# The end of a decoder step on one core: one tile's residual to GpSimd, the samples' output to GpSimd, and the last tile's additions in another order

## The reference

```python
xp = xp + mp[5] * hierarchical_moe(modulate(xp, norm_ffn_g[l], mp[3], mp[4]), ...)
xs = xs + ms[5] * hierarchical_moe(modulate(xs, norm_ffn_g[l], ms[3], ms[4]), ...)
```

## Time and profile before

| | |
|---|---|
| median of 3 runs | 760.4 us (759.92 to 761.41) |
| the profiled execution, span | 768.8 us |
| TensorE busy | 739.2 us (96%) |
| VectorE busy | 409.4 us (53%) |
| ScalarE busy | 205.8 us (27%) |
| GpSimd busy | 171.1 us (22%) |
| mean granted TensorE clock | 0.990 |
| read from and written to memory | 180.89 MB and 16.13 MB |

### The profile page before, as it was taken

How to read it: one execution, slowest core, us unless ns; L and a number is a source line. 1 busy time by engine, 2 the same in 40 slices (tenths; PEclk the granted TensorE clock), 3 DMA queues, 4 the chain that set the end, 5 groups by cost and what they waited for, 6 DMA issues and landing times.

```text
span 768.8 us, 11131 instructions
## 1 busy us (share of the span) xinstructions
PE 739.2 (96%) x4235; PEld 464.7 (60%) x4235; DVE 409.4 (53%) x942; ACT 205.8 (27%) x418; POOL 171.1 (22%) x193
## 2 busy tenths in 40 slices
PE   7999999999999999998999999989999999999986
PEld 5445465688756567885888444656555555555541
DVE  4124399998999998600254235974432232222235
ACT  5012253306467675002000011222111111111112
POOL 2031021240000000073400004543333333333210
PEclk9999999999999999998999999989999999999999
DMA  8973064113255275443232842377999999999988
GB/s 339 419 254 97 0 218 159 46 78 115 109 220 220 110 256 207 143 166 138 80 116 83 344 179 92 139 260 286 423 423 425 427 424 423 426 426 422 423 332 321
DMA packets 29385, 187.72 MB, mean 244 GB/s; under 512 B 7264, under 2 KB 8352, under 8 KB 17936
## 3 DMA queue, kind: packets, MB, share of 16 engines
q1 hardware_dynamic: 18880, 164.98, 53.9%
q0 software_dynamic: 9536, 19.72, 7.8%
q10 hardware_dynamic: 912, 2.26, 0.8%
HBM read 180.89 MB, written 16.13 MB: 256 GB/s over the span
## 4 chain that ended last, share of the span: by engine, by line
PE 75%; DVE 9%; DMA 8%; issue 3%; ACT 2%; SPq 1%; POOL 1%; DVEq 0%; ACTq 0%; POOLq 0%
PE psum L810 23%; PE psum L1302 13%; PE psum L777 12%; PE psum L1316 7%; DMA ring<-in_experts 5%; PE psum L724 3%; PE psum L1295 2%; DMA ring<-in_stream 2%; PE psum L670 2%; DMA ring<-expert_rows 1%; DVE arena L2284 1%; DVE arena L2282 1%; DVE arena L2283 1%; PE psum L653 1%; PE psum L1309 1%
## 5 line engine op out<-in xcount | busy, mean ns | idle before, releaser
L810 PE MATMUL psum<-hT,ring 128*128 128x260 f32 x640 | 146.7, 389 | 5.3 <-issue 3.3
L810 PEld LDWEIGHTS psum<-hT,ring 128*128 128x128 f32 x640 | 121.9, 192 | 29.5 <-issue 8.5
L1785 ACT ACTIVATE arena<-psum 128x512 f32<-128x512 f32 (+10 forms) x127 | 68.3, 573 | 234.8 <-PE psum L653 50.9
L777 PE MATMUL psum<-ring,hT 128*128 128x512 f32 (+1 forms) x256 | 93.1, 517 | 0.0
L777 PEld LDWEIGHTS psum<-ring,hT 128*128 128x128 f32 x256 | 47.4, 190 | 41.8 <-issue 32.6
L1302 PE MATMUL psum<-ring,arena 128*64 128x256 f32 x608 | 69.0, 379 | 2.2 <-DMA ring<-in_experts 1.2
L1316 PE MATMUL psum<-arena 128*64 128x512 f32 x280 | 67.8, 605 | 1.4 <-issue 1.4
L1717 POOL DMA_INDIRECT expert_rows<-arena,router x34 | 34.5, 1014 | 140.0 <-DVE arena L2784 127.7
L1302 PEld LDWEIGHTS psum<-ring,arena 128*64 128x64 f32 x608 | 43.8, 137 | 31.3 <-issue 10.3
L2777 DVE COPY arena<-psum 128x128 f32<-128x128 f32 x35 | 10.2, 291 | 95.6 <-PE psum L1309 83.8
L810 PE MATMUL psum<-arena,ring 128*128 128x260 f32 x256 | 58.9, 386 | 0.0
(11 more groups left out here) (398 smaller groups left out, 962.5 us busy)
## 6 DMA issues: line engine op xcount, KB each, us to landing
ring<-in_stream SPq DMA_DIRECT2D x21, 2048.0 KB, 8.9
ring<-in_experts SPq DMA_DIRECT2D x16, 2048.0 KB
arena<-in_experts SPq DMA_DIRECT2D x32, 1024.0 KB
arena<-in_experts SPq DMA_DIRECT2D x11, 2048.0 KB
hT<-in_experts SPq DMA_DIRECT2D x5, 2048.0 KB
ring<-expert_rows SPq DMA_DIRECT2D x8, 512.0 KB, 7.2
ring<-in_stream SPq DMA_DIRECT2D x2, 1280.0 KB, 6.1
arena<-in_x_prompt SPq DMA_DIRECT2D x4, 512.0 KB, 5.7
```

Of the source, the lines that this page charges most:

```text
L777: mm = pe.matmul(psum[:, b, 0:width], hT[:, k, t * P:(t + 1) * P], w[:, k, :], start=(k == 0), stop=(k == KD - 1))
L810: mm = pe.matmul(psum[:, b0 + s, 0:HALF], w[:, k, f * P:(f + 1) * P], rhs[:, k, s * HALF:(s + 1) * HALF], start=(first and k == 0), stop=( ...
L1785: ins = act.activation(out, in_, func, scale=scale)
```

## The change

- TensorE: the residual of tile 1 no longer goes through PSUM; its sums start with the first one-hot matmul. The residual half in the wait for `y_out` is now one of tile 2.
- ScalarE copies tile 1's sums to `last_sums`, free space in `hT`, so that `x2[:, 1, :]` keeps the residual.
- GpSimd, behind its overflow loop, adds `picked[1][1]` to `x2[:, 1, :]`; VectorE adds `last_sums` to `picked[0][1]`, waits for GpSimd, and adds `x2[:, 1, :]`.
- VectorE: in the last tile, the PSUM sums and the second choices are added first, as soon as both are there, and then, in two halves, the first choices.
- GpSimd waits for its scatter, loads the samples' two choices, does the three small operations and stores `y_s`; then it waits for that store. SyncE no longer does any of this, and VectorE neither.
- Two semaphores are shared with others than before.

```diff
@@ TensorE
             down(LAST_P, w_dn[k], y_full)
-            last_residual(1, 0)
+            last_residual(2, 0)
             pe.wait_ge(last_hot_ready, 3)
             pe.wait_ge(y_out, N_MAIN)
             last_tile(0)
-            last_residual(1, 1)
+            banks.begin(pe, ("last", 1), LAST_BANK[1], LAST_BANK[1] + 1)
             last_tile(1)
-            for h in range(2):
-                last_residual(2, h)
+            last_residual(2, 1)
             last_tile(2)
@@ last_rows
-                                 start=False, stop=True)
+                                 start=(t == 1), stop=True)
@@ SyncE
-                if t == 1:
-                    sp.wait_ge(*s_scattered)
-                    for c in range(2):
-                        sp.dma_start(s_cols[:, 2 + c, :], sample_columns(by_token[c, SEQ:TOK, :])).then_inc(s_picked[0], 16)
...
-            sp.wait_ge(*y_s_ready)
-            sp.dma_start(sample_columns(io["y_s"]), s_cols[:, 2, :]).then_inc(y_outs, 16)
-            sp.wait_ge(y_outs, 16 * (T5 + 1))
+            sp.wait_ge(y_outs, 16 * T5)
@@ GpSimd, behind over_pairs
+            pool.wait_ge(*picked_in[1][1])
+            lane.mark(pool.tensor_tensor(x2[:, 1, :], x2[:, 1, :], picked[1][1], ALU.add))
+            x2_picked.append(lane.count)
+            pool.wait_ge(*s_scattered)
+            for c in range(2):
+                pool.dma_start(s_cols[:, 2 + c, :], sample_columns(by_token[c, SEQ:TOK, :])).then_inc(s_picked[0], 16)
+            a, gate2, x = s_cols[:, 2, :], s_cols[:, 0, :], s_cols[:, 1, :]
+            pool.wait_ge(*s_back)
+            pool.wait_ge(*s_picked)
+            lane.then(pool.tensor_tensor(a, a, s_cols[:, 3, :], ALU.add))
+            lane.then(pool.tensor_tensor(a, a, gate2, ALU.mult))
+            lane.then(pool.tensor_tensor(a, a, x, ALU.add))
+            store(sample_columns(io["y_s"]), a)
             pool.wait_ge(outs, 16 * n_outs[0])
@@ ScalarE
-                evac(("last", t), [(halves(x2[:, t, :]), psum[:, LAST_BANK[t]:LAST_BANK[t] + 2, :])])
+                sums = last_sums if t == 1 else x2[:, t, :]
+                evac(("last", t), [(halves(sums), psum[:, LAST_BANK[t]:LAST_BANK[t] + 2, :])])
@@ VectorE
-            for t in range(NT):
-                picks_summed(t)
-                if t < NT - 1:
-                    last_added(t)
+            picks_summed(0)
+            last_added(0)
+            dve.wait_ge(*picked_in[0][1])
+            banks.wait_drained(dve, ("last", 1))
+            lane.then(dve.tensor_tensor(picked[0][1], picked[0][1], last_sums, ALU.add))
+            dve.wait_ge(pool_lane, x2_picked[0])
+            dve.tensor_tensor(picked[0][1], picked[0][1], x2[:, 1, :], ALU.add).then_inc(y_ready, 1)
+            picks_summed(2)
+            last_added(2)
+            t = NT - 1
+            dve.wait_ge(*picked_in[1][t])
+            for h in range(2):
+                banks.wait_drained(dve, ("last", t, h))
+            lane.then(dve.tensor_tensor(x2[:, t, :], x2[:, t, :], picked[1][t], ALU.add))
+            dve.wait_ge(*picked_in[0][t])
             for h in range(2):
                 cols = slice(512 * h, 512 * h + 512)
-                banks.wait_drained(dve, ("last", t, h))
-                if h == 0:
-                    lane.wait()
                 dve.tensor_tensor(picked[0][t][:, cols], picked[0][t][:, cols], x2[:, t, cols], ALU.add).then_inc(y_ready, 1)
-
-            a, gate2, x = s_cols[:, 2, :], s_cols[:, 0, :], s_cols[:, 1, :]
-            dve.wait_ge(*s_back)
-            dve.wait_ge(*s_picked)
-            lane.then(dve.tensor_tensor(a, a, s_cols[:, 3, :], ALU.add))
-            lane.then(dve.tensor_tensor(a, a, gate2, ALU.mult))
-            dve.tensor_tensor(a, a, x, ALU.add).then_inc(y_s_ready[0], 1)
```

More of the change, by code:

```diff
@@ L432, in decoder_step @@
         s_cols = at(19456, 4 * Q_S).rearrange("p (m n) -> p m n", m=4)
+        last_sums = hT.rearrange("p k n -> p (k n)")[:, 0:D]
         last_hot = at(20992, NT * P).rearrange("p (t n) -> p t n", t=NT)
@@ L500, in decoder_step @@
         s_kept = (c_in, 16 + 32)
-        const2_in = sem("const2_then_s_picked_in")
-        s_picked = (const2_in, 32 + 32)
+        const2_in = sem("const2_in")
         bias_gain_in = sem("bias_gain_in_then_spread_moved")
@@ L533, in decoder_step @@
         x2_in = [(sem("x2_0_in"), 16), (ln_in, 32), (ws_in, 32), (pages_in, 32), (pages_all_in, 32)]
-        router_in = sem("router_in")
+        router_in = sem("router_then_s_picked_in")
+        s_picked = (router_in, 32 + 32)
         x2_half, x2_ready = sem("x2_half"), sem("x2_ready")
@@ L580, in decoder_step @@
         max_s_ready, probs_s_ready = sem("max_s_ready"), sem("probs_s_ready")
-        new_spread_ready = sem("new_spread_then_y_s_ready")
-        y_s_ready = (new_spread_ready, 2)
+        new_spread_ready = sem("new_spread_ready")
         merged = sem("merged")
@@ L585, in decoder_step @@
         vector_lane, scalar_lane, pool_lane = sem("vector_lane"), sem("scalar_lane"), sem("pool_lane")
-        n_outs = [0]
+        n_outs, x2_picked = [0], []
         last_use = {}
```

## The result

The changed kernel is slower: 773.27 us median of 17 runs against 763.56 us for the kernel before on the same chips, ratio 1.0126 (95% interval 1.0107 to 1.0145), that is 9.6 us more (8.2 to 11.1). The forecast was 11.4 us more: right in sign and in cause, and 1.8 us too large. As a time it was 771.8 us, only 1.5 us from the measured one, and that closeness is luck: it was added to the 760.4 us of three runs, which lie 3.2 us under the median of all 17.

The account below looks back on a forecast made before the run. It took the end to be bound by the prompt's last half and the samples, within 0.2 us. `y_s` at 770.1 plus GpSimd's uncovered drain gave +11.4 us; added to 760.4 that is 771.8 us, range 760.5 to 775.0.

Parts of the forecast that it names:

- the sum: Kernel's end: `y_s` lands at 770.1, then GpSimd's whole drain, to 780.2 us, 11.4 over the profiled 768.8.
- the blocked VectorE addition: Tile 1's first VectorE addition, held by GpSimd's; claimed to end 1.06 us behind it, at 759.8.
- The drain: GpSimd's close: the whole 9.64 us, as fixed work over all issued, runs uncovered behind `y_s`; chance 0.53.
- rival (a): GpSimd's close: the drain settles something for 4.7 us behind the last landing; +6.3, 766.7 us; chance 0.12.
- (b): GpSimd's close: the drain costs nothing when the queue is empty; +1.7, 762.1 us; chance 0.24.
- The sample path: End of GpSimd: sample loads, three additions and store land `y_s` at 770.1, about 1.7 us later than before.
- The collision: Tile 1: GpSimd's and VectorE's additions don't run side by side; VectorE's halves end at 766.1, 0.7 us later.
- its twin: GpSimd's 1024-wide addition in the router stage, 2.35 us, taken as the length of the new one.
- The gain: TensorE about 2 us shorter; the last tile's new order alone gains VectorE 1.3 us.

Follow-up runs that it names:

- e10: The kernel before plus one wait: GpSimd waits for all stores of y before it closes; ratio 1.0114 to the kernel before.
- e9: The changed kernel with two early GpSimd drains in idle stretches, behind the load of `b_router` and behind the last full scatter; ratio 1.0011 to the kernel before.
- e4: The changed kernel, but SyncE stores `y_s` once GpSimd's last operation is done; ratio 1.0103 to the kernel before.
- e7: The changed kernel with two early GpSimd drains, before the wait for the tables and behind the last full scatter; ratio 1.0059 to the kernel before.
- e1: The kernel before with only the samples' loads, sums and store moved to GpSimd; ratio 1.0141 to the kernel before.
- e5: The changed kernel with 64 more one-element transfers issued by GpSimd in an idle stretch; ratio 1.0135 to the kernel before.
- e6: The changed kernel with one early GpSimd drain, before the wait for the tables; ratio 1.0097 to the kernel before.
- e3: The changed kernel with samples back on SyncE and VectorE, and VectorE adding tile 1's residual instead of GpSimd; ratio 0.9990 to the kernel before.
- e2: The changed kernel with the samples given back to SyncE and VectorE, GpSimd's 1024-wide addition kept; ratio 1.0007 to the kernel before.

## Why the prediction was right

| term of the sum, us | predicted | measured |
|---|---|---|
| VectorE's last half ready, against before | +0.7 | +0.45 |
| GpSimd's addition / the blocked VectorE addition | 2.35 / ends 1.06 behind it | 2.89 / ends 1.08 behind it |
| last half's store to landing | 2.7 | 2.1 |
| second sample load landed, behind the scaling | 13.2 | 12.4 |
| three operations on GpSimd, to the store's issue | 1.7 | 2.6 |
| store of `y_s` to landing | 2.5 | 1.8 |
| `y_s` landed, behind the scaling | 17.4 | 16.8 |
| closing drain | 9.65 | 8.07 |
| TensorE's last matmul, against before | -2 | -2.1 |
| end of the span, against before | +11.4 | +9.5 |

**The drain.** The step that carried the forecast, that the 9.64 us of the earlier trace rows are work over what was issued and not a wait, held: e10 shows it with nothing of the change, e9 by taking it away. The prediction chose this reading by elimination, from one row, and gave it 0.53; and its range, 760.5 to 775.0 us, took in rival (a) and most of (b), so the runs, and not the time in the range, bear it out. Its size was the mis-sized term, by 1.6 us. The prediction called it work over all that was issued, and in that it was wrong: with three transfers more the drain was shorter, 8.07 us against 9.30 in e10, and with 64 more on top it stayed so. Why is open. Rival (a) read the 4.7 us behind the scatter's landing in the kernel before as a settlement; e4 refutes it. Rival (b), the free drain, is what e7 and e9 make of it when they leave four transfers: then the end is 1.5 to 1.6 us later than before by the trace, a ratio of 1.002; timed, e9 has 1.0011, and e7 1.0059 with its badly placed first drain. The Trainium skill (VectorE: DVE Perf Modes, The DRAIN you can't avoid) gives about 12 ns for such drains on all five engines. For SyncE (13) and ScalarE (8) the traces agree. The rows of TensorE (8 to 702) and VectorE (264 to 1332) are longer, but where they are, they end within 0.1 us of the engine's last operation. For GpSimd, after it issued transfers, the traces show 391 to 9698 ns.

**The sample path.** 0.6 us shorter than in the sum, by three errors that partly cancel: the loads landed 0.8 us and the store 0.7 us sooner than the rows I took, and the three operations up to the store's issue took 0.9 us more, most of it the 0.8 us between GpSimd's last operation and its store, which I had not counted (it was 0.83 us in e1 too, and 0.29 in e5, e6, e7 and e9). No run shows the cause of either; in e1 GpSimd waited 4.82 us for the same loads and not 3.35. The bounds of the forecast have two slips: the lower one, 769.3, takes 767.6 as the landing of `y_s`, where the sum of the lowest terms is 766.6 (768.3 us in time), and the upper one adds 2.6 us for the operations, where 3 was the bound given (775.0).

**The collision.** It came as forecast, at its place and with its end. GpSimd's addition was 0.5 us longer than its twin; it began 0.7 us ahead of the end of the VectorE addition in front (749.20 to 750.43), and so was itself held first, as the sum had it. That VectorE's last half came out 0.25 us better is spread over the steps: GpSimd's addition and the blocked one ended 0.1 us sooner behind the scaling than in the sum, and the six additions behind them took 0.1 us less. VectorE's first sum has no part in it: in e5 it waited 0.42 us for its load, and the last half was ready at 13.2 us all the same.

**The gain.** By the trace TensorE's shorter work and the new order do bring something: e3, which has both without GpSimd's addition, ends 15.0 us behind the scaling against 16.1. The timed runs give 0.9990 (0.9969 to 1.0011), so it can't be told from nothing. No kernel of this study is measurably faster than the one before.

**How the profile could have misled.** By spans alone the change would have cost 3.5 us, and e2 and e3 would have gained 11 and 9. The 8.4 us between the span of before and its timed median, which the prediction carried over, are of the same kind: in every later profile the span is 1.7 to 1.9 us shorter than the time of its own execution, so the profiled execution of the kernel before, whose own time is not on record, was most likely a long one.

## What to carry to other kernels

Look at how every engine closes: a drain that ends unseen under other work has a length, and a change that makes its engine the last one brings it to the end in full. On GpSimd that length grows with the transfers issued since its last drain, so let GpSimd come to its close some 10 us before the others do, whatever its last work is (e10 has no transfer there, and e4 stores from SyncE), or place a drain in an idle stretch ahead of its last transfers, where it delays neither a gather nor a scatter. And an addition given to GpSimd is not parallel work while VectorE adds from SBUF.

## What the runs showed of the hardware

- GpSimd's drain takes by itself 0.06 us and 0.083 us for each transfer that GpSimd has issued since the last drain (seen for 4, 58, 63, 70, 74 and 75 transfers). For more it was shorter than that: 9.3 us for 134, 9.5 for 136, and 8.07 for 137 and for 201.
- An indirect scatter's issue is held by a VectorE addition with two SBUF inputs. The last scatter starts 0.83 to 0.85 us behind the scaling in all twelve profiles, VectorE's first addition at different times, and the scatter's length varies with it from 1.15 to 1.75 us so that it always ends 0.85 or 0.86 us behind that addition. In e3:

```profile
744.45 1.23 DVE L2839 TENSOR_TENSOR ring<-ring 128x1024 f32<-128x1024 f32 x1
```

```profile
745.21 1.32 POOL L1738 DMA_INDIRECT expert_rows<-arena,router  x1 [7.47 <-DVE arena L2785]
```

745.68 to 746.53 is 0.85 us; in the kernel before 754.46 to 755.31 is 0.85 too, and in e5 746.18 to 747.03. The Trainium skill (SBUF — State Buffer, Who interferes with whom) infers that descriptor generation isn't held by a `tensor_tensor`. For the plain loads that GpSimd issues the traces agree: 0.58 and 0.61 us each in the changed kernel while VectorE adds, and 0.53 to 0.86 for the plain ones elsewhere in the kernel before. For the indirect one they don't. Which part of its work is held wasn't tried.
